# Weight tiles interleaved column by column, and the buffers of moving operands rebased modulo 256 bytes

## What is computed

```python
def swiglu(h, w_in, w_out):
    gate, up = jnp.split(h @ w_in, 2, axis=-1)
    return (jax.nn.silu(gate) * up) @ w_out
...
def hybrid_layer(x, w_in, ...):
    h = rms_norm(x, norm_w)
    p = h @ w_in
    ...
    proj = jnp.einsum('bsgc,gcd->bsgd', branches, w_branch)
    gates = jax.nn.sigmoid(merge.reshape(bsz, seq, N_BRANCHES, D_MODEL).astype(jnp.float32))
    mixed = jnp.sum(gates * proj, axis=2)
    return x + (mixed @ w_out).astype(x.dtype)
```

## Time and profile before

| | before |
|---|---|
| median of the runs | 2420.63 us (2419.8 to 2421.6) |
| span of the profiled execution | 2419.5 us |
| matmuls, weight loads | 14712, 14712 |
| PE busy | 2384.9 us, 99% |
| weight loads (PEld) busy | 2059.6 us, 85% |
| DVE, ACT busy | 1600.1 us (66%), 1063.2 us (44%) |
| DMA | 346.53 MB, mean 143 GB/s |
| mean granted TensorE clock | 0.997 |

### The profile page before, as it was taken

The page is one execution under the profiler, slowest core; times in us unless marked ns, Lnnn a source line. Parts: engine busy times, 40 slices in busy tenths (PEclk is TensorE's granted clock), DMA queues, the critical chain, the costliest instruction groups (busy, mean ns, idle before and its releaser), DMA issues.

```text
span 2419.5 us, 36353 instructions
## 1 busy us (share of the span) xinstructions
PE 2384.9 (99%) x14712; PEld 2059.6 (85%) x14712; DVE 1600.1 (66%) x2899; ACT 1063.2 (44%) x1882; POOL 0.2 (0%) x4
## 2 busy tenths in 40 slices
PE   9999999999999999999999999999999999999998
PEld 5888888976788888888888888899998998999997
DVE  7776775477587677377623357655586776877767
ACT  4222324455552223252223245644556556555663
POOL 0000000000000000000000000000000000000000
PEclk9999999999999999999999999999999999999999
DMA  6554552211125455215522212245534443444432
GB/s 275 207 195 188 202 198 70 88 53 53 71 91 197 186 198 203 87 55 207 207 107 90 102 70 88 111 157 181 191 142 157 175 140 127 167 169 158 157 123 88
DMA packets 48408, 346.53 MB, mean 143 GB/s; under 512 B 5361, under 2 KB 5489, under 8 KB 6769
## 3 DMA queue, kind: packets, MB, share of 16 engines
q1 hardware_dynamic: 48242, 344.21, 38.3%
HBM read 343.14 MB, written 1.05 MB: 142 GB/s over the span
## 4 chain that ended last, share of the span: by engine, by line
PE 92%; DVE 5%; ACT 2%; issue 1%; DMA 0%; SPq 0%; DVEq 0%; ACTq 0%
PE ps L484 26%; PE ps L485 25%; PE ps L486 25%; PE ps L826 1%; PE ps L828 1%; PE ps L827 1%; DVE w_lo L2119 1%; PE ps L873 1%; PE ps L1030 1%; PE ps L654 1%; ACT w_hi L1430 1%; PE ps L679 1%; PE ps L1056 1%; PE ps L859 1%; PE ps L608 1%
## 5 line engine op out<-in xcount | busy, mean ns | idle before, releaser
L1430 ACT ACTIVATE w_hi<-ring 128x1024 fp32r<-128x1024 f32 x494 | 523.4, 1060 | 1052.5 <-PE ps L486 988.9
L2119 DVE TENSOR_TENSOR w_lo<-ring,w_hi 128x1024 fp32r<-128x1024 f32 x494 | 603.5, 1223 | 422.8 <-ACT w_hi L1430 419.5
L484 PE MATMUL ps<-u_hi,w_hi 128*128 128x512 f32 (+1 forms) x1856 | 656.8, 354 | 4.8 <-DVE u_lo L2192 2.3
L485 PE MATMUL ps<-u_lo,w_hi 128*128 128x512 f32 (+1 forms) x1856 | 648.6, 349 | 0.0
L486 PE MATMUL ps<-u_hi,w_lo 128*128 128x512 f32 (+1 forms) x1856 | 648.4, 349 | 0.0
L484 PEld LDWEIGHTS ps<-u_hi,w_hi 128*128 128x128 f32 x1856 | 348.4, 188 | 60.9 <-issue 7.7
L485 PEld LDWEIGHTS ps<-u_lo,w_hi 128*128 128x128 f32 x1856 | 348.5, 188 | 47.3 <-issue 0.5
L486 PEld LDWEIGHTS ps<-u_hi,w_lo 128*128 128x128 f32 x1856 | 348.6, 188 | 45.5
L484 PE MATMUL ps<-uh,w_hi 128*128 128x256 f32 x1136 | 321.9, 283 | 2.9 <-DVE w_lo L2119 1.7
L2107 DVE CUSTOM_DVE_ANT_0 waste<-ring,condb,cols 128x1024 f32<-128x1024 f32 x260 | 322.3, 1279 | 0.1
L486 PE MATMUL ps<-uh,w_lo 128*128 128x256 f32 x1136 | 315.4, 278 | 0.0
(11 more groups left out here) (364 smaller groups left out, 2686.6 us busy)
## 6 DMA issues: line engine op xcount, KB each, us to landing
ring<-in_wk SPq DMA_DIRECT2D x317, 1024.0 KB, 4.8
mix<-in_wk SPq DMA_DIRECT2D x3, 1024.0 KB, 16.2
yT<-in_wk SPq DMA_DIRECT2D x2, 1024.0 KB, 7.8
hT<-in_x SPq DMA_DIRECT2D x1, 2048.0 KB, 13.1
htabs<-in_htabs SPq DMA_DIRECT2D x1, 1088.0 KB, 7.3
out_t<-uT SPq DMA_DIRECT2D x2, 512.0 KB, 2.6
trig<-in_trig SPq DMA_DIRECT2D x3, 256.0 KB, 7.5
wuk<-in_uk SPq DMA_DIRECT2D x2, 256.0 KB, 5.1
```

Source lines behind the costliest of these rows:

```text
L484: mm(bank, hi, x_hi, start=first, stop=False, skip_group_check=skip)
L485: mm(bank, hi, x_lo, start=False, stop=False, skip_group_check=skip)
L1430: f(half_hi(K, 0, HALF), ringed(n, K % 2 * HALF, (K % 2 + 1) * HALF), ACT.Copy).then_inc(whi_ready, 1)
L2119: tt(half_lo(K, 0, HALF), ringed(HALF_SLOT[K], K % 2 * HALF, (K % 2 + 1) * HALF), half_hi(K, 0, HALF).bitcast(F32), ALU.subtract).then_inc ...
```

## The change

Three things are changed. On the host, the tiles of a half are interleaved in pairs: column c of tile 2i and column c of tile 2i + 1 are neighbours. Halves with tiles of 256 columns stay as they are. In the kernel, every call of `three` takes its weights through `tile_hi(h, k)` and `tile_lo(h, k)`, which read every second float over 255 of them; `values` and both conversions keep `half_hi` and `half_lo`. And the regions of the blocks begin at new places: the first block's at a multiple of 256 bytes behind `w_hi` (192 bytes later than before), the second block's 192 bytes after that, which is 192 modulo 256. The number, order, shapes and waits of all instructions and DMAs stay the same.

```diff
@@ -41,6 +41,10 @@
 NRING = 4
+
+LINE = 256
+U_APART = 0
+SECOND_APART = 192
...
@@ -168,6 +172,7 @@
         ring = place("fixed", "ring", NRING * SLOT)
+        first_half = at["fixed"]
...
-        phases = at["fixed"]
+
+        def apart(place, distance):
+
+            return place + (distance - (place - first_half)) % LINE
+
+        phases = apart(at["fixed"], U_APART)
...
-        at["second"] = phases
+        at["second"] = apart(phases, SECOND_APART)
...
+        def tile_hi(h, k):
+            n = (h % NW) * HALF + k // 2 * 2 * P + k % 2
+            return w_hi[:, n:n + 2 * P - 1:2]
+
+        def tile_lo(h, k):
+            n = (h % NW) * HALF + k // 2 * 2 * P + k % 2
+            return w_lo[:, n:n + 2 * P - 1:2]
...
@@ -516,7 +534,7 @@
-                    last = three(bank[:, 0:T], half_hi(H, k * P, (k + 1) * P), half_lo(H, k * P, (k + 1) * P),
+                    last = three(bank[:, 0:T], tile_hi(H, k), tile_lo(H, k),
                                  xh[:, at_k], xl[:, at_k], k == 0, k == KC - 1)
...
@@ -2945,6 +2963,9 @@
             to[...] = w[:, c0:c1].reshape(k, P, width).transpose(1, 0, 2)
+            if width != 2 * P:
+                to = self.a[self.n, :, at:at + k * width].reshape(P, -1, P, 2)
+                to[...] = to.reshape(P, -1, 2, P).transpose(0, 1, 3, 2).copy()
```

More of the change, by code:

```diff
@@ L581, in two_columns @@
                     for b in range(2):
-                        last = three(banks[b][:, 0:T], half_hi(H + b, k * P, (k + 1) * P),
-                                     half_lo(H + b, k * P, (k + 1) * P), xh[:, at_k], xl[:, at_k], k == 0, k == KC - 1)
+                        last = three(banks[b][:, 0:T], tile_hi(H + b, k),
+                                     tile_lo(H + b, k), xh[:, at_k], xl[:, at_k], k == 0, k == KC - 1)
                         if k == KC - 1:
@@ L910, in block @@
                 def block(b, k):
-                    last = three(banks[b][:, :], half_hi(H + b, k * P, (k + 1) * P),
-                                 half_lo(H + b, k * P, (k + 1) * P), u_hi[:, k * TT:(k + 1) * TT],
+                    last = three(banks[b][:, :], tile_hi(H + b, k),
+                                 tile_lo(H + b, k), u_hi[:, k * TT:(k + 1) * TT],
                                  u_lo[:, k * TT:(k + 1) * TT], k == 0, k == KC - 1)
@@ L1167, in _ @@
                         for b in range(2):
-                            last = three(pair[b][:, 0:S], half_hi(H + b, k * P, (k + 1) * P),
-                                         half_lo(H + b, k * P, (k + 1) * P), tile(lead_hi, k), tile(lead_lo, k),
+                            last = three(pair[b][:, 0:S], tile_hi(H + b, k),
+                                         tile_lo(H + b, k), tile(lead_hi, k), tile(lead_lo, k),
                                          k == 0, k == KC - 1)
@@ L1387, in _ @@
                             for k in range(4):
-                                last = three(bank, half_hi(H, (t * 4 + k) * P, (t * 4 + k + 1) * P),
-                                             half_lo(H, (t * 4 + k) * P, (t * 4 + k + 1) * P),
+                                last = three(bank, tile_hi(H, t * 4 + k),
+                                             tile_lo(H, t * 4 + k),
                                              tile(br_hi[p], k), tile(br_lo, BR_AT[p] + k), k == 0, k == 3)
```

12 lines of the change are left out of this document (6 added, 6 removed).

## The result

The changed kernel is slower: 2472.23 us, the median of four runs (2469.51 to 2473.08), against 2420.22 for the kernel before beside it. The ratio is 1.0217, with a 95% interval of 1.0202 to 1.0231. The forecast was 2321 us, in a range of 2303 to 2385.

The account below looks back on a forecast made before the run. TensorE's matmul issue was taken as the bound. Gains of 63.7 us (512 columns) and 46.9 (256), less 6.4, 2.4 and 2.3, gave 99.5 us: 2321 us forecast, range 2303 to 2385, of which 2303 to 2345 had 0.57.

Parts of the forecast that it names:

- The floor: Least time per fp32r matmul in `three`, taken from plain float32: 215.6 ns for 512 columns, 109.0 for 256; full gain 110.6 us.
- what that something is: Step explaining 15.5 ns extra per long matmul and 6.6 to 11.1 per short one by weight and moving readers clashing.
- Equal speed: Interleaved weight loads walk 8 bytes per 0.83 ns, as fast as fp32r moving operands, so neither reader overtakes the other.
- third rival: The strided weight load is slower and holds up short matmuls; up to 3060 us at twice the load time; chance 0.12.
- turning point: Load time at which slower strided loads turn the change into a loss: some 122 ns, 15% longer.
- The meetings: In `three`'s streams, the two readers clash whenever they meet modulo some distance; one pace per number of meetings.
- the rival that one stays: One meeting per matmul remains in one or both blocks; everywhere, gain 54.6 us, time 2366 us; chance 0.23.
- The loads take no part: Rival: the excess belongs to reading fp32r itself, so the change does nothing, 2420.6 us; chance 0.08.
- The cover in the feed-forward stretches: Term (c): in the feed-forward, conversions, VectorE and weight loading from memory stay hidden behind the matmuls, so nothing is deducted.
- the window of 330 us: Pure feed-forward stretch, expected to shrink in proportion to the gain, from 330 to about 311 us.
- (a): Deduction for clashes that stay in `three`'s streams: one matmul in eight, 6.4 us, between bounds of 0 and 51.3.
- (b): Deduction where others set the pace: 2.4 us in the first block's attention, 2.3 us in the second block.

Follow-up runs that it names:

- small kernel: Kernels without the blocks, running only streams of `three`'s kind of matmul, other engines idle; fp32r never under 226.7 ns (512 columns) or 113.3 (256).

## Why the prediction was wrong

**The floor, wrong, and with it the gain.** The step that failed is the one under "what that something is": that plain float32 matmuls, which lose nothing beside a load of equal speed, show what an fp32r matmul can reach. They don't. Plain float32 takes 215.8 ns for 256 columns and needs 64 lines in it; at 1.77 ns a line that is 113 ns, so it has half its time to spare, and a loss in fetching need not show. A contiguous fp32r operand needs a line every 1.67 ns (512 columns in 213.3 ns at the 2.4 GHz level, four columns a line), which is faster than one every 1.77, so it has nothing to spare. Its floor is 128 lines x 1.77 = 226.6 ns and 64 x 1.77 = 113.3, and no small kernel goes below 226.7 and 113.3, whatever was loaded. Against it before loses 2.3 ns on a long and 2.9 on a short matmul (229.0 and 116.2 in the table): 4824 x 2.3 = 11.1 and 7104 x 2.9 = 20.6 us, some 32 us in all where I counted 110.6. The rest was never there to win. The floor itself is measured. That the fetching of lines makes it is an inference: one price fits plain steps 2, 3 and 4, fp32r with step 2 in the moving operand within 1%, and fp32r's floor, and at half the clock, where a line is needed only every 3.33 ns, the excess is gone (426.7 ns). Nothing shows the fetches themselves.

**"Equal speed" by the wrong measure, and the third rival.** I counted bytes walked per ns, where what counts is lines fetched per ns. A load side by side fetches 32 lines, interleaved 64. The same price gives a lower bound for it, 64 lines in 113.3 ns; back to back it takes 117.8 (L115) where it was 112.4 (L114), and with step 4, 128 lines or 226.6 ns, it takes 233.3, so loads come out 3 to 4% above the price. The interleaved load is thus a bound of 117.8 ns for a short matmul, 1.6 over before's 116.2, which is 11 us of the +27.0 in the table. The other 2.2 ns, 16 us, lie above that bound. How they come about no run shows. Already beside step-2 loads of 64 and 32 columns (L99, L100), which they can't be waiting for, short matmuls take 116.7 and 117.3 ns against 113.3 with step 1, so the wait for the load is not the whole of it. This was the third rival, given 0.12. Its direction was right and its signs came nearly as written: load records over 188 ns (195) and short matmuls at 120.0, where it had over 120. Its turning point, a load of some 122 ns, was wrong because it set the loss against a gain of 64 us on the long matmuls, of which at most 11 were there. The Trainium skill (SBUF — State Buffer, the note on cachelines) says that two hits in a 16-byte line keep full bandwidth, and I let it speak against this rival. Its line of 16 bytes agrees with the runs; its two hits don't: with two a plain moving operand went from 215.8 to 225.0 ns, a load from 112.4 to 117.8, and an fp32r moving operand from 113 to 120 up to 228.5. The measurement decides.

**The 512 columns, +27.5 us: shown where, not why.** A load of 117.8 ns fits almost twice into 227, so waiting for it can't set this pace. The relative place does: with step 2 the small kernel and the whole one agree at 64 (233.3) and at 192 (230.1); at 0 it is 233.3 in the small kernel and 233.3 and 235.5 in the two windows of after. With step 1 it is 226.7 at 0 and 228.9 at 64. Over all 16 distances the two steps are nearly equal (231.8 and 232.6 ns in the mean), but before stood at one of the few good ones for its step and after does not. Why the pace settles above the floor, and why it does so at one place and not at another, stays open. That it is no plain clash with the load is shown by loads of 2 columns: 231.1 at 64 and 231.7 at 0, slower than with full loads.

**The meetings, and the rival that one stays.** The two stable paces of the earlier trace rows come back in small kernels with every other engine idle, so VectorE, ScalarE and the DMAs aren't needed for them, as I had said of the first two. The rows themselves were a weaker witness than I made of them: by the groups of the two windows the first holds matmuls of `u_hi` and `u_lo` alone and the second those of `h_hi` and `h_lo`, equal modulo 256 but different buffers. It is the small kernels that show both paces for one and the same operands (113.3 and 117.8 ns at 64). But they are no "number of meetings" to be got rid of by equal speed: the forecast's sign, one pace of 215.6 and one of 109 ns for the two widths, was met nowhere in fp32r. The rival's 2366 us fell with the same floor.

**The loads take no part** was given 0.08, and holds for most of the excess: of the 15.5 ns of a long matmul 13.4 belong to fp32r itself. It doesn't hold for what is above it. At distance 0 a short matmul takes 113.3 ns with 2-column loads (L98, as at 64) and 120.0 with full ones (L94). The Trainium skill (SBUF — State Buffer, section "Who interferes with whom") has two independent ports for the two operands; this difference speaks against their independence, if the ports are where it arises.

**The rest of the sum.** The counts, the conversions (1061 and 1223 ns) and the DMA volume stayed, as said. The cover in the feed-forward stretches held; the window of 330 us did not shrink to 311 but holds fewer matmuls (1416 records where it was 1453), because they got longer. Terms (a) and (b), shares of a gain that didn't come, have nothing to be held against. `values` was taken as 0, within 3.9 us either way: it cost 2.9 + 0.8 = 3.7 us, and since the kernel with contiguous weights and the new distances also shows 119.9 ns in the first block, that part comes with the distance alone. With the interleaving at the old distances it was 116.3 ns against 113.9, though nothing about its own operands had changed; what that comes from stays open.

## What to carry to other kernels

Before a gain is counted against a floor, the floor has to be measured on the same kind of operand: one stream of the matmul in question with a 2-column load beside it would have shown 113.3 instead of 109 ns, and with twice as much, 226.7, for the long ones the gain would have come to 26 us instead of 110.6. As a working rule from these runs, count the 16-byte lines that a reader touches in the time it has: contiguous fp32r has none to spare, and a weight load beside 256-column matmuls only as long as its columns lie side by side. The relative place of weights and activations is worth some per cent of a stream, in jumps, with opposite signs for different shapes; a small kernel at multiples of 64 bytes is a fair guide to it, but it showed two paces itself at 64 and 192 with 256 columns, and the place has to be tried in the whole kernel.

## What the runs showed of the hardware

Not expected: the time of a strided TensorE read goes by the 16-byte lines that it touches, some 1.77 ns for each in the moving operand (225.0, 339.0 and 451.9 ns for 128, 192 and 256 lines) and 3 to 4% more in a load (117.8 and 233.3 ns for 64 and 128); the line is inferred from these times and from the loads with steps 4 and 8. At 2.4 GHz no fp32r stream here took under 226.7 ns a matmul with 512 columns or under 113.3 with 256, while plain float32 reaches 215.8 with 256 columns; in the slow start of a trace 512 columns took 426.7 ns, without any excess. The paces above the floor depend on the operands' relative place, both within 16 bytes (231.9, 236.9, 233.3 and 229.3 ns in the mean at 0, 4, 8 and 12 past a multiple, 512 columns) and beyond, and at some places on something that the address alone doesn't fix (226.8 or 236.6 at 240 with 512 columns, 113.3 or 117.8 at 64 with 256). What that is wasn't settled.
